# One hand-ordered run of weight units up to the second block, with the later modulation products moved into the feed-forward part

## The chip, the cores and the metric

One core of a Trainium2 chip runs the whole program in one launch. The metric is the device time in microseconds, from the first to the last instruction of an execution, as the median of several executions. Engines: PE is TensorE (matrix products), ACT is ScalarE, DVE is VectorE, POOL is GpSimd, SP issues most transfers. SBUF is the on-chip memory, PSUM the eight banks into which PE writes.

## What is computed

Two model blocks on 256 tokens of width 2048, in float32. The first block is

    a = rms_norm(x); z = a @ w_in                     # 2048 x 4656
    y = concat(rms_norm(rglru(z)), rms_norm(nsa(z)))  # recurrent part and sparse attention
    h = x + rms_norm(y @ w_out)
    f = square(relu(rms_norm(h) @ mlp_w1)) @ mlp_w2   # 2048 x 8192 and back
    h = h + rms_norm(f)
    h = h + sigmoid(h @ ple_gate) * (p @ ple_proj)

and the second has two layers, each on 256 tokens of h and 256 context tokens:

    shift, scale, gate = split(silu(c) @ w_mod[l] + b_mod[l], 3)     # one row for h, one for the context
    z = (rms_norm(x) * (1 + scale) + shift) @ w_in_2[l]              # 2048 x 6656
    y = concat(diff_attention, multiscale_pool, conformer_conv) @ w_out_2[l]
    x = x + gate * y

The modulation vectors depend on `c` and `c_ctx` alone, so their products with `w_mod` (2 x 2048 x 6144) can be made at any time before they are needed.

## The kernel before, in words

**Weight units.** Every large product is cut into chunks of 512 output columns, and each chunk into four units. A unit is a 1 MB piece of weights (512 rows by 512 columns), which SP loads into one of four buffers `raw`. ACT rounds it to `whi` (L1096, L1104, L1352), DVE makes the remainder `wlo = raw - whi` (L1535, L1542, L1900), and PE makes 24 matmuls of 128x128 by 512 from it (4 row tiles, 2 token tiles, and hi*hi, hi*lo, lo*hi; L615 to L617 in `unit`, L656 to L658 in `hand_unit`, L905 to L907 in the feed-forward part). `whi` and `wlo` have two buffers, so ACT may round unit n+1 when PE has used unit n-1. A buffer of `raw` is free when its `wlo` is made (`lo_ready`), and SP then loads the unit four places on.

**Preparation.** `prep` turns normed rows into the stationary operand: PE transposes two column tiles to PSUM (L601), DVE copies them to `tmp` with the column scale (L1527, L1529), ACT rounds that to `hi` (L1089) and POOL subtracts to `lo` (L2141), in 8 groups of 128x512. PE may write the PSUM bank again when DVE has copied it (`t_tmp`).

**Order of the stages.** `HAND` is an order of units written out by hand: 40 units of `in1` with 32 modulation units of layer 0 between them (L742, followed once in five units by a column sum, L732), then 52 units of the context's input product `in2_0c` beside the sparse attention. Modulation units are used by PE straight from `raw`: four fp32 matmuls with 32 columns each, in four column strips of the array. Behind `HAND` the stages follow with a barrier of four engines (`boundary`, L412) between them: `out1` (16 units), the norm and residual `post` (L1139, L1608, L1610) and `prep("mlp")`, the feed-forward part `mlp` (128 units as a loop over four quarters), `post` again, `prep("ple")`, the product with `ple_proj` (L928, fp32), `gate` (16 units), a norm and `prep("m2_00")`, `in2_0` (52 units), and layer 0 of the second block. In `quarter` the rows of the first product are squared by POOL (L2218), transposed by PE (L879) and split by ACT and DVE (L1342, L1873).

**The attention of layer 0** runs 32 batches (L984, L1009, L996 on PE; L1414, L1424 on ACT; L2011, L2024, L2031 on DVE). Between them DVE makes the 31 taps of the convolution (L1991, L1993; one tap a batch in layer 0, two in layer 1), POOL multiplies the gate by its gain once (L2245), and PE makes the remaining 16 groups of modulation products, four units each (`mod_products`, L671), each followed by ACT's copy (L1145), a sum over the strips on PE (`mod_total`, L678), ACT's copy of the row (L1151) and POOL's store to DRAM (L2159). `load_mod` brings the rows of layer 1 back (L2165) to be transposed (L940).

Of the kernel before, what the change touches and what calls it, by code (L numbers as in the profile page):

```python
# [91 lines left out]
def build(nc, I, out):  # L92
    ctx = ExitStack()
    with ctx:
# [27 lines left out]
        vmod = flip[0:64, :]  # L122
        stat = sb("stat", [P, 16])
        epsc = sb("epsc", [P, 1])
# [12 lines left out]
        with region(0) as st:  # L137
# [13 lines left out]
            pT = zst[:, 0, TB].rearrange("p (k t) -> p k t", k=2)  # L151

# [62 lines left out]
        with ExitStack() as st:  # L215
# [12 lines left out]
            modp_b = sb("modp_b", [P, CH], F32, st)  # L228
            modst_b = sb("modst_b", [2, 2, CH], F32, st)
# [31 lines left out]
        class Phase:  # L261
# [10 lines left out]
            Phase("out1", w_out1, 0, 4, 2, "y"),  # L272
            Phase("mlp", None, 0, 8 * FF_Q, 2, "mlp"),
            Phase("pp", None, 0, 4, 2, "pp", split=False),
            Phase("gate", w_gate, 0, 4, 2, "gate"),
            Phase("in2_0", w_in2[0], 0, 13, 2, "z"),
            Phase("mod1", None, 0, len(MODB), 1, "modb", split=False),
# [8 lines left out]
        for ph in PH:  # L286
            ph.r0, ph.s0, ph.c0, ph.z0, ph.p0 = r, s, c, zc, pu
            ph.count = {"s0": s, "c0": c, "z0": zc}
            units = 4 if ph.kind in ("cmp", "pp") else 4 * ph.chunks
            r += units  # L290
            s += units if ph.split else 0
            pu += 0 if ph.split else units
            c += 0 if ph.kind in ("cmp", "mod", "modb", "kept") or ph.name == "in2_0c" else ph.chunks
            zc += ph.chunks if ph.kind == "z" else 0
        BY = {ph.name: ph for ph in PH}

        def after(name, what):
# [9 lines left out]
            dict(name="mix1", src=h, kt=KT, rms=True, mat=eye, xn=xb, hi=ax_hi, lo=ax_lo, off=0, tmp=tmp,  # L307
# [6 lines left out]
                 tmp=G[:, :, :, :].rearrange("p a b c -> p (a b c)")[:, 0:8 * SEQ].rearrange("p (s k t) -> p s k t", k=2, t=SEQ),  # L314
                 scale=lambda k: cols[:, C_GNSA + k:C_GNSA + k + 1], shift=None, units=after("in1g", "s0")),
            dict(name="mlp", src=h, kt=KT, rms=True, mat=eye, xn=xb, hi=ax_hi, lo=ax_lo, off=0, tmp=tmp,
                 scale=lambda k: cols[:, C_MLPPRE + k:C_MLPPRE + k + 1], shift=None, units=after("out1", "s0")),
            dict(name="ple", src=h, kt=KT, rms=False, mat=eye, xn=h, hi=ax_hi, lo=ax_lo, off=0, tmp=tmp,
                 scale=lambda k: ones[:, 0:1], shift=None, units=after("mlp", "s0")),
        ]  # L320
        for l, sm in ((0, 0), (1, 0), (1, 1)):
# [7 lines left out]
        t, nr = 0, 0  # L329
        for pr in PREPS:  # L330
            pr["t0"], pr["r0"] = t, nr
            t += pr["kt"] // 2
            nr += 1 if pr["rms"] else 0
# [10 lines left out]
        class Unit:  # L344

            def __init__(self, ph, i, u, r, s, p):
                self.ph, self.i, self.u, self.r, self.s, self.p = ph, i, u, r, s, p
                self.slot, self.landed = r % UPC, 16 * (r // UPC + 1)

        def laid(order, r, done):  # L350

            out_ = []
            for name in order:
                ph = BY[name]
                k = done.get(name, 0)
                done[name] = k + 1
                out_.append(Unit(ph, k // UPC, k % UPC, r + len(out_), ph.s0 + k if ph.split else None,
                                 None if ph.split else ph.p0 + k))
            return out_

        beside_in1 = []
        for n in range(40):
            beside_in1 += ["in1" if n < 36 else "in1g"] + (["mod0"] if n % 5 < 4 else [])
        beside_nsa = ["in2_0c"] * 4 + ["cmp", "in2_0c"] * 4 + ["in2_0c"] * 44
        done_units = {}
        FIRST = laid(beside_in1, 0, done_units)
        SECOND = laid(beside_nsa, len(FIRST), done_units)
        HAND = FIRST + SECOND
        IN1 = [x for x in FIRST if x.s is not None]
        MOD0 = [x for x in FIRST if x.s is None]  # L370
        CTX0 = [x for x in SECOND if x.s is not None]
        CMP = [x for x in SECOND if x.s is None]
        assert len(HAND) % UPC == 0 and len(HAND) == BY["out1"].r0

        def half(x, b):

            a = (2 * x.i if x.ph.name == "in1" else 18 if x.ph.name == "in1g" else 20 + 2 * x.i) + b
            return a, a % 3
# [108 lines left out]
        for n in ("vec_T", "vec_cols", "cvec_ready", "bias_psum", "bias_row", "bias_out", "lam_dot", "lam_exp",  # L487
                  "lam_ready", "mod_in", "mod_T", "mod_part", "mod_sum", "mod_row", "modp_in", "modc_sum", "modc_set", "x_again", "cvec_zero", "c_T0", "c_copy0",
                  "uc_ready", "pT_psum", "pT_ready", "p_in", "h_in", "lru_w", "bd_zero",
                  "uT_pad", "lru_T", "gT_ready", "xc_ready", "lru_gates", "lru_sig", "lru_ln", "lru_sp", "lru_exp",  # L490
                  "lru_q", "lru_sqrt", "lru_y", "lru_ysq", "lru_ss", "lru_rms", "lru_yn", "lru_hi", "lru_lo",
# [16 lines left out]
        def _(sp):  # L508
# [14 lines left out]
            for n, x in enumerate(HAND):  # L523
# [6 lines left out]
                if x.ph.kind == "cmp":  # L530
                    src = I["cmp_w1_k" if x.u < 2 else "cmp_w1_v"][0].rearrange("(k p) n -> p k n", p=P)
                    sp.dma_start(raw[:, x.slot].rearrange("p a b -> p (a b)").rearrange("p (k n) -> p k n", n=256),
                                 src[:, 8 * (x.u % 2):8 * (x.u % 2) + 8, :]).then_inc(raw_in[x.slot], 16)
                else:
                    sp.dma_start(raw[:, x.slot, :, 0:x.ph.width], x.ph.w[:, UK * x.u:UK * x.u + UK, wcols(x.ph, x.i)])\
                      .then_inc(raw_in[x.slot], 16)
            for ph in PH[PH.index(BY["out1"]):]:
                if ph.kind == "modb":
                    for m_, (l, col) in enumerate(MODB):
                        for u in range(UPC):  # L540
                            free(ph, m_, u)
                            sp.dma_start(raw[:, u], w_mod[l][:, UK * u:UK * u + UK, col * CH:col * CH + CH]).then_inc(raw_in[u], 16)
                elif ph.kind == "pp":
                    for u in range(4):
                        free(ph, 0, u)
                        sp.dma_start(raw[:, u, 0:2, :], I["ple_proj"][0].rearrange("(k p) n -> p k n", p=P)[
                            :, :, u * CH:u * CH + CH]).then_inc(raw_in[u], 16)
                elif ph.kind == "mlp":
                    def quarter(q, first):
                        for j in range(8):  # L550
                            for u in range(UPC):
                                if first and j == 0:
                                    free(ph, 0, u)
                                else:
                                    sp.wait_ge(lo_ready, q * 32 + (ph.s0 + 4 * j - UPC + u + 1))
                                if j < 4:
                                    src = w_up[:, UK * u:UK * u + UK, bass.ds(q * D + j * CH, CH)]
                                else:
                                    src = w_down[:, bass.ds(q * KT + UK * u, UK), (j - 4) * CH:(j - 3) * CH]
                                sp.dma_start(raw[:, u], src).then_inc(raw_in[u], 16)  # L560
                    quarter(0, True)
                    with sp.Fori(1, FF_Q) as q:
                        quarter(q, False)
                else:
# [18 lines left out]
        def _(pe):  # L583
            mm = nc.tensor.matmul

            def prep(name, groups=None):

                if name == "ple":
                    pe.wait_ge(ev("post_done"), 4)
                for g in groups or steps(name):  # L590
# [3 lines left out]
                    if n >= 4:  # L594
                        pe.wait_ge(t_tmp, n - 3)
# [1701 lines left out]
```

## Time and profile before

| what | us |
|---|---|
| median of 3 runs (lowest, highest) | 3214.56 (3213.85, 3218.7) |
| the profiled execution | 3217.97 |
| its span | 3216.3 |
| PE busy | 2849.1 (89%) |
| DVE busy | 1656.3 (51%) |
| ACT busy | 1132.1 (35%) |
| POOL busy | 181.2 (6%) |
| bytes moved, mean rate | 589.21 MB, 183 GB/s |

A busy time is a union over the instructions of an engine, so overlapping matmuls are counted once. The profiled execution took 1.7 us more than its span.

### The profile page before, as it was taken

To read this page: it belongs to the slowest core of one execution; us is meant where nothing else is said; L and a number is where in the kernel's file an instruction comes from. 1 tells how busy PE (TensorE), PEld (TensorE's weight loads), DVE (VectorE), ACT (ScalarE), POOL (GpSimd) and SP (SyncE) were. 2 spreads that over 40 slices of the span, in tenths; PEclk is the share of its full clock that TensorE was granted. 3 is DMA by queue.
4 is the path that set the end of the run, shared out by engine and by line. 5 is a ranking of instruction groups with operands and counts; after the bars stand their busy time and mean duration, and the time that the engine had idled before them with its cause. 6 is when DMAs were issued, how large, how long until landed. Compare 5 with 4: busy or idle time off the path is not lost. (4 is left out here: it accounts for less than half of the span.)

```text
span 3216.3 us, 33116 instructions
## 1 busy us (share of the span) xinstructions
PE 2849.1 (89%) x13308; PEld 2232.7 (69%) x13308; DVE 1656.3 (51%) x1821; ACT 1132.1 (35%) x1321; POOL 181.2 (6%) x176
## 2 busy tenths in 40 slices
PE   4999899998799999999798999787599799996568
PEld 3777788887588888888586887332288678784356
DVE  3644556654554544444544444797533522346954
ACT  3452344433433333333334332343311411232433
POOL 2000100000100000000101000010000200000000
PEclk9999899999899999999899999799799899997789
DMA  6867464464455555555354666799243233464033
GB/s 206 281 236 254 152 232 154 155 223 167 138 187 189 191 187 189 188 187 190 130 190 150 222 221 204 297 339 377 86 149 103 98 128 118 151 221 172 0 135 131
DMA packets 284887, 589.21 MB, mean 183 GB/s; under 512 B 13522, under 2 KB 21562, under 8 KB 282192
## 3 DMA queue, kind: packets, MB, share of 16 engines
q1 hardware_dynamic: 261088, 512.13, 47.1%
q0 software_dynamic: 11552, 48.25, 4.0%
q10 hardware_dynamic: 12112, 26.91, 2.3%
q8 instruction: 100, 1.64, 0.2%
q14 instruction: 35, 0.29, 0.0%
HBM read 560.41 MB, written 26.84 MB: 183 GB/s over the span
## 5 line engine op out<-in xcount | busy, mean ns | idle before, releaser
L1535 DVE TENSOR_TENSOR wlo<-raw,whi 128x2048 fp32r<-128x2048 f32 x170 | 389.0, 2291 | 624.0 <-ACT whi L1096 623.6
L1096 ACT ACTIVATE whi<-raw 128x2048 fp32r<-128x2048 f32 x170 | 325.0, 1915 | 758.1 <-PE ps L617 731.9
L615 PE MATMUL ps<-whi,ax_hi 128*128 128x512 f32 x1344 | 530.4, 395 | 44.8 <-DVE wlo L1535 19.3
L616 PE MATMUL ps<-wlo,ax_hi 128*128 128x512 f32 x1344 | 527.8, 393 | 0.0
L617 PE MATMUL ps<-whi,ax_lo 128*128 128x512 f32 x1344 | 527.5, 392 | 0.0
L1900 DVE TENSOR_TENSOR wlo<-raw,whi 128x2048 fp32r<-128x2048 f32 x126 | 288.8, 2292 | 360.9 <-ACT whi L1352 360.9
L1352 ACT ACTIVATE whi<-raw 128x2048 fp32r<-128x2048 f32 x126 | 241.5, 1917 | 444.9 <-PE ps L907 444.9
L1542 DVE TENSOR_TENSOR wlo<-raw,whi 128x2048 fp32r<-128x2048 f32 (+1 forms) x92 | 203.0, 2207 | 283.5 <-ACT whi L1104 283.2
L615 PEld LDWEIGHTS ps<-whi,ax_hi 128*128 128x128 f32 x1344 | 256.0, 190 | 101.7 <-issue 41.0
L1104 ACT ACTIVATE whi<-raw 128x2048 fp32r<-128x2048 f32 (+1 forms) x92 | 169.8, 1845 | 386.7 <-PE ps L658 229.7
L616 PEld LDWEIGHTS ps<-wlo,ax_hi 128*128 128x128 f32 x1344 | 256.0, 190 | 52.9
L617 PEld LDWEIGHTS ps<-whi,ax_lo 128*128 128x128 f32 x1344 | 255.2, 190 | 53.8
L905 PE MATMUL ps<-whi,ax_hi 128*128 128x512 f32 x512 | 200.7, 392 | 1.9 <-issue 1.9
L905 PE MATMUL ps<-whi,ay_hi 128*128 128x512 f32 x512 | 199.6, 390 | 0.0
L907 PE MATMUL ps<-whi,ax_lo 128*128 128x512 f32 x512 | 199.5, 390 | 0.0
L907 PE MATMUL ps<-whi,ay_lo 128*128 128x512 f32 x512 | 199.3, 389 | 0.0
L906 PE MATMUL ps<-wlo,ax_hi 128*128 128x512 f32 x512 | 199.2, 389 | 0.0
L906 PE MATMUL ps<-wlo,ay_hi 128*128 128x512 f32 x512 | 199.2, 389 | 0.0
L656 PE MATMUL ps<-whi,ay_hi 128*128 128x512 f32 x416 | 167.4, 402 | 6.0 <-DVE wlo L1542 6.0
L658 PE MATMUL ps<-whi,ay_lo 128*128 128x512 f32 x416 | 163.9, 394 | 0.0
L657 PE MATMUL ps<-wlo,ay_hi 128*128 128x512 f32 x416 | 163.5, 393 | 0.0
L1993 DVE SCALAR_TENSOR_TENSOR bv<-uc,cols,bv 128x512 f32<-128x512 f32 (+1 forms) x240 | 140.8, 649 | 0.5
(372 smaller groups left out, 4036.5 us busy)
## 6 DMA issues: line engine op xcount, KB each, us to landing
raw<-in_w_in_dram SPq DMA_DIRECT2D x192, 1024.0 KB, 5.1
raw<-in_mlp_w_dram SPq DMA_DIRECT2D x128, 1024.0 KB, 5.2
raw<-in_w_mod_dram SPq DMA_DIRECT2D x96, 1024.0 KB, 8.5
raw<-in_w_out_dram SPq DMA_DIRECT2D x48, 1024.0 KB, 5.0
raw<-in_ple_gate_dram SPq DMA_DIRECT2D x16, 1024.0 KB, 5.0
z<-zst POOLq DMA_DIRECT2D x22, 512.0 KB, 4.7
z<-zsc POOLq DMA_DIRECT2D x13, 512.0 KB, 3.2
h<-in_x_dram POOLq DMA_DIRECT2D x2, 2048.0 KB, 10.8
```

Of the source, the lines that this page charges most:

```text
L615: mm(dst, hi_[:, kk, tt], whi[:, u % 2, k, 0:width], start=(kk == 0), stop=False)
L616: mm(dst, hi_[:, kk, tt], wlo[:, u % 2, k, 0:width], start=False, stop=False)
L617: ins = mm(dst, lo_[:, kk, tt], whi[:, u % 2, k, 0:width], start=False, stop=(kk == KT - 1))
L905: mm(dst, hi_[:, kk, tt], whi[:, u % 2, k], start=(kk == 0), stop=False)
L906: mm(dst, hi_[:, kk, tt], wlo[:, u % 2, k], start=False, stop=False)
L907: ins = mm(dst, lo_[:, kk, tt], whi[:, u % 2, k], start=False, stop=(kk == KT - 1))
L1096: A(whi[:, u % 2, :, 0:width], raw[:, u, :, 0:width], ACT.Copy).then_inc(hi_ready, 1)
L1104: A(whi[:, x.s % 2, :, 0:w], raw[:, x.slot, :, 0:w], ACT.Copy).then_inc(hi_ready, 1)
L1352: A(whi[:, u % 2], raw[:, u], ACT.Copy).then_inc(hi_ready, 1)
L1535: V.tensor_tensor(wlo[:, u % 2, :, 0:ph.width], raw[:, u, :, 0:ph.width], f32v(whi[:, u % 2, :, 0:ph.width]), ALU.subtract).then_inc(lo_re ...
L1542: V.tensor_tensor(wlo[:, x.s % 2, :, 0:w], raw[:, x.slot, :, 0:w], f32v(whi[:, x.s % 2, :, 0:w]), ALU.subtract).then_inc(lo_ready, 1)
L1900: V.tensor_tensor(wlo[:, u % 2], raw[:, u], f32v(whi[:, u % 2]), ALU.subtract)\
```

## The change

- The hand-written order now runs on to the end of `in2_0`: 48 units of `in2_0c`, the 16 of `out1`, the last 4 of `in2_0c`, the 128 of `mlp` with the 64 modulation units of `mod1` among them (after four of every seven feed-forward units, for 16 x 7 = 112 units), then four times one unit of `ple_proj` and four of `gate`, then the 52 of `in2_0`. The feed-forward loop is written out. The barriers between these stages are gone, and each accumulator of 128x512 is read out by itself, in a ring of three PSUM banks.
- `post` is replaced: ACT squares each chunk as it is read out (`squares`, `down_squares`, `row_squares`), DVE sums and inverts (`rms`), ACT takes the root (`root`), and DVE adds the residual by chunks (`residual`). The norm ahead of `mlp` is applied behind the first product, as the scale `rinv` in its read-out. POOL multiplies the rows of the second norm by their gain. The transposes of `prep("mlp")` stand among the last four units of `in2_0c`.
- `prep` of `mix1`, `nsa`, `mlp` and `ple` has no `tmp`: ACT writes `hi` from PSUM and DVE `lo` from PSUM; POOL has no part. In every `prep`, PE now waits for `a_lo` instead of `t_tmp`.
- The modulation columns of layer 1 are set from PSUM as those of layer 0 are (8 column sums of 4 small matmuls); only the 8 gate rows still go to DRAM. Nothing of `mod1` is left in the attention.

The core of the diff:

```diff
-        beside_nsa = ["in2_0c"] * 4 + ["cmp", "in2_0c"] * 4 + ["in2_0c"] * 44
+        order += ["in2_0c"] * 4 + ["cmp", "in2_0c"] * 4 + ["in2_0c"] * 40
+        order += ["out1"] * 16 + ["in2_0c"] * 4
+        for n in range(128):
+            order += ["mlp"] + (["mod1"] if n < 7 * len(MODB) and n % 7 in (0, 1, 3, 4) else [])
+        order += (["pp"] + ["gate"] * 4) * 4 + ["in2_0"] * 52
...
                     if n >= 4:
-                        pe.wait_ge(t_tmp, n - 3)
+                        pe.wait_ge(a_lo, n - 3)
...
+            for n, x in enumerate(CTX0[48:]):
+                hand_unit(x, AY_)
+                if n in (1, 2):
+                    turned("mlp", 2 * n - 2, 0)
+                    turned("mlp", 2 * n - 1, 0)
...
+                hand_unit(x, AX_ if j < 4 else AY_)
+                m_, at = n // 7, n % 7
+                if m_ < len(MODB) and at in (0, 1, 3, 4):
+                    if at == 0 and m_:
+                        pe.wait_ge(ev("modc_set"), MODSS + before(COLS, m_))
+                        pe.wait_ge(ev("mod_row"), before(ROWS, m_))
+                    mod_products(MOD1[4 * m_ + (0, 1, 0, 2, 3)[at]], 3)
+                elif m_ < len(MODB) and at == 5:
+                    pe.wait_ge(ev("modp_in"), MODSS + m_ + 1)
+                    if m_ in COLS:
+                        mod_columns(modp_b, 3)
+                    else:
+                        mm(ps[0:2, 3, :], sel[:, :], modp_b, start=True, stop=True).then_inc(ev("modc_sum"), 1)
...
+            for i in range(4):
+                turned("ple", i, 4)
+            pe.wait_ge(ev("pT_ready"), 1)
+            for x in GATE:
+                if x.i == 0:
+                    pe.wait_ge(a_lo, PR["ple"]["t0"] + 2 * (x.u + 1))
+                hand_unit(x, AY_)
+                if x.u == 2:
+                    y = PP[x.i]
...
+            pe.wait_ge(gate_mul, 8)
+            for i in range(4):
+                turned("m2_00", i, 8)
+            for x in X0:
+                if x.i == 0:
+                    pe.wait_ge(a_lo, PR["m2_00"]["t0"] + 2 * (x.u + 1))
+                hand_unit(x, AX_)
             boundary(pe, 0)
...
-                    if l == 0 and n and n % 2 == 0 and n <= 2 * len(MODB):
-                        mod_total(n // 2 - 1, modp_b)
...
-                    if l == 0 and n < 2 * len(MODB):
-                        mod_products(n // 2, (0, 1) if n % 2 == 0 else (2, 3))
-                pe.wait_ge(ev("mod_row"), len(MODB))
```

## Rows read from the trace of the kernel before

**Rows 1.** Windows by stage: window, length, PE, PEld, DVE, ACT, POOL, PEclk, DMA, GB/s.
```profile
725.20:735.60 10.40, 1.00 (x6) 0.53 (x4) 3.14 (x3) 3.71 (x2) 0.72 (x1) 0.75 0.13 51
735.60:825.20 89.60, 89.60 (x384) 73.68 (x384) 37.53 (x18) 26.82 (x14) 0.00 (x0) 0.97 0.56 188
825.20:854.40 29.20, 5.60 (x33) 5.57 (x33) 22.27 (x24) 15.30 (x19) 3.31 (x4) 0.59 0.31 108
854.40:1568.20 713.80, 711.88 (x3203) 589.67 (x3201) 345.51 (x180) 258.60 (x146) 37.63 (x22) 1.00 0.56 183
1568.20:1608.60 40.40, 21.45 (x69) 12.91 (x69) 25.48 (x30) 13.35 (x16) 11.19 (x10) 0.78 0.37 129
1698.30:1718.80 20.50, 6.91 (x33) 5.52 (x32) 14.21 (x18) 12.92 (x14) 2.59 (x3) 0.70 0.26 90
2047.40:2241.70 194.30, 156.79 (x961) 57.78 (x961) 165.33 (x327) 86.81 (x262) 18.85 (x20) 0.94 0.98 362
```
**Rows 2.** Timeline of PE in the first stage: start, us, engine, line.
```profile
162.37 1.07 PE L742 MATMUL ps<-raw,cvec 128*32 128x512 f32 x8
163.37 0.50 PE L656 MATMUL ps<-whi,ax_hi 128*128 128x512 f32 x1
...
170.03 0.50 PE L656 MATMUL ps<-whi,ax_hi 128*128 128x512 f32 x1
...
259.77 0.50 PE L656 MATMUL ps<-whi,ax_hi 128*128 128x512 f32 x1
...
266.16 0.48 PE L656 MATMUL ps<-whi,ax_hi 128*128 128x512 f32 x1
```
**Rows 3.** Timeline of DVE in the feed-forward part.
```profile
873.07 2.29 DVE L1900 TENSOR_TENSOR wlo<-raw,whi 128x2048 fp32r<-128x2048 f32 x1 [3.15 <-ACT whi L1352]
878.51 2.29 DVE L1900 TENSOR_TENSOR wlo<-raw,whi 128x2048 fp32r<-128x2048 f32 x1 [3.15 <-ACT whi L1352]
```
**Rows 4.** Groups of instructions: count, busy us, mean ns, idle before and its releaser.
```profile
L678 PE MATMUL ps<-modp_b,sel 128*2 128x512 f32 x32 | 18.0, 647 | 0.7 <-ACT modp_b L1145 0.6
L928 PE MATMUL ps<-raw,zst 128*128 128x512 f32 x32 | 13.9, 592 | 0.0
L671 PE MATMUL ps<-raw,cvec 128*32 128x512 f32 x512 | 68.8, 630 | 21.5 <-DMA raw<-in_w_mod_dram 18.9 <-ACT modst_b L1151 1.8
```
**Rows 5.** Timeline of the attention of layer 0.
```profile
2072.26 0.75 DVE L2024 SCALAR_TENSOR_TENSOR e<-e,st 128x512 f32<-128x512 f32 x1
...
2077.61 0.75 DVE L2024 SCALAR_TENSOR_TENSOR e<-e,st 128x512 f32<-128x512 f32 x1
...
2140.98 11.60 DVE L1993 SCALAR_TENSOR_TENSOR bv<-uc,cols,bv 128x512 f32<-128x512 f32 x4
2141.15 8.88 POOL L2245 TENSOR_TENSOR k<-k,subg 128x4096 f32<-128x4096 f32 x1
...
2153.73 0.48 DVE L2024 SCALAR_TENSOR_TENSOR e<-e,st 128x256 f32<-128x256 f32 x1
...
2158.28 0.48 DVE L2024 SCALAR_TENSOR_TENSOR e<-e,st 128x256 f32<-128x256 f32 x1
...
2226.55 0.69 DVE L2011 TENSOR_REDUCE st<-ps 128x2 f32<-128x512 f32 x1 [0.94 <-PE ps L984]
...
2236.24 0.35 DVE L2031 TENSOR_SCALAR q<-ps,st 128x128 f32<-128x128 f32 x1 [1.10 <-PE ps L996]
```
**Rows 6.** A window of layer 1's attention, which has no modulation products.
```profile
2980.00:3000.00 20.00, 13.16 (x57) 8.20 (x55) 19.55 (x47) 6.67 (x21) 0.00 (x0) 0.66 0.00 0
```
**Rows 7.** Timeline of a preparation with POOL.
```profile
336.25 10.01 POOL L2141 TENSOR_TENSOR ay_lo<-zsc,ay_hi 128x512 fp32r<-128x512 f32 x8 [0.64 <-ACT ay_hi L1089]
```
**Rows 8.** SP's issues behind the product of 162.37, and the rounding they allow.
```profile
163.91 0.51 SPq L535 DMA_DIRECT2D raw<-in_w_in_dram  x1
...
172.52 1.92 ACT L1104 ACTIVATE whi<-raw 128x2048 fp32r<-128x2048 f32 x1 [8.07 <-DMA raw<-in_w_in_dram]
```
**Rows 9.** DMA issues by tensor: count, KB each, median us to landing.
```profile
raw<-in_mlp_w_dram SPq DMA_DIRECT2D x128, 1024.0 KB, 5.2
```

More of the change, by code:

```diff
@@ new lines, in build, with of @@
+        HAND = laid(order)
+        SPLIT = [x for x in HAND if x.s is not None]
+        def of(name):
+            return [x for x in HAND if x.ph.name == name]
+        IN1, MOD0, CTX0, CMP, PP = of("in1") + of("in1g"), of("mod0"), of("in2_0c"), of("cmp"), of("pp")
+        MOD1 = of("mod1")
+        OUT1, MLP, GATE, X0 = of("out1"), of("mlp"), of("gate"), of("in2_0")
+        assert len(HAND) % UPC == 0 and len(HAND) == BY["out2_0"].r0
+        ROWS = [m_ for m_, (l, col) in enumerate(MODB) if col >= MODSS]
@@ L536, in _ @@
                       .then_inc(raw_in[x.slot], 16)
[L537 to L564, printed above, removed]
+            for ph in PH[PH.index(BY["out2_0"]):]:
+                if ph.chunks:
                     def body(i, odd, ph=ph):
@@ L1324, in _ @@
             beside = Beside(nsa())
[L1325 removed]
+            for n, x in enumerate((CTX0[0:48] + OUT1[0:2])[2:]):
                 hand_split(x)
                 beside(n)
[L1328 to L1338 removed]
@@ L1355, in _, with squares @@
-            quarter(0, True)
-            with act.Fori(1, FF_Q) as q:
-                quarter(q, False)
-            boundary(act, 1)
-            post(1, yb, after("mlp", "c0"))
-            prep("ple")
-            gemm("gate", gate=True)
+            def squares(xs, i, n):
+                for b in range(TB):
+                    a, bank = half(chunk(xs, i)[0], b)
+                    act.wait_ge(unit_used, chunk(xs, i)[3].s + 1) if b else act.wait_ge(half_done, a // 2 + 1)
+                    A(yb[:, b, i * CH:i * CH + CH], ps[:, bank, :], ACT.Square, accum_out=ssq[:, n, b, i:i + 1])\
+                        .then_inc(ev("post_sq"), 1)
@@ new lines, in _, with sigmoids @@
+            hand_split(GATE[0])
+            down_squares(3)
+            root(2)
+            hand_split(GATE[1])
+            prep("ple")
+            def sigmoids(i):
+                for b in range(TB):
+                    a, bank = half(chunk(GATE, i)[0], b)
+                    act.wait_ge(unit_used, chunk(GATE, i)[3].s + 1) if b else act.wait_ge(half_done, a // 2 + 1)
+                    if i >= 2:
+                        act.wait_ge(gate_mul, 2 * (i - 2) + b + 1)
+                    A(zst[:, i % 2, b], ps[:, bank, :], ACT.Sigmoid).then_inc(half_out, 1)
@@ new lines, in _ @@
+            for n, x in enumerate((OUT1 + CTX0[48:] + MLP[0:2])[2:]):
+                if n < 16 and n % 4 == 3:
+                    gained(n // 4)
+                if n == 19:
+                    to_memory(CTX0, 12)
+                hand_low(x)
+                if n == 15:
+                    rms(0, 0, 8)
+                    dve.wait_ge(ev("x_again"), 16)
+                    residual(0, 0)
+                    residual(0, 1)
+                if n == 16:
+                    residual(0, 2)
+                    residual(0, 3)
+                if n in (17, 18):
+                    prep("mlp", range(4 * n - 68, 4 * n - 64))
```

708 lines of the change are left out of this document (371 added, 337 removed).

## The prediction

> **What bounds the kernel now.** Read the windows by stage first [rows 1]. In the feed-forward part (854.4 to 1568.2) PE is busy 711.9 of 713.8 us at the full clock of 2.4 GHz (PEclk 1.00): whatever is added to PE's stream there lengthens the run by its whole price. Between the stages lie holes in which PE does little: 10.4 us ahead of `out1`, 29.2 ahead of `mlp`, 40.4 ahead of `gate`, 20.5 ahead of `in2_0`. Layer 0's attention (194.3 us) is another kind of stage: PE 156.8 us, DVE 165.3 us. Its timeline [rows 5] decides which of the two sets the pace. Where nothing is late, DVE's step at L2024 recurs every 5.35 us (2072.26 to 2077.61) for the batches of 512 keys and every 4.55 us (2153.73 to 2158.28) for those of 256, and DVE has no idle time ahead of these rows. So over long stretches the modulation products run beside DVE's work for nothing. The change fills the holes, which is a gain, and takes 64 products from a stage in which most of them are free to one in which none is.
>
> **The cost of the products on PE.** The first stage already mixes weight units and products in this manner. From 163.37 to 170.03 there is one unit and one product, 6.66 us [rows 2]; a unit alone has a pitch of 5.44 us, 873.07 to 878.51 [rows 3]. One product costs 1.22 us: 64 x 1.22 = 78.1 us. A unit with a column sum takes 266.16 - 259.77 = 6.39 us [rows 2], so a sum costs 0.95 us: 8 x 0.95 = 7.6. The 8 row sums are two records of L678 each, 18.0 us for 16 of them [rows 4], 1.1 us, and I add 0.2 us for entering and leaving as the product shows (1.22 against 68.8 / 64 = 1.08 busy [rows 4]): 8 x 1.3 = 10.4. The four transposes of `p`, until now in a hole, go in too: about 1.1. Together 97.2 us. Bounds: 90 (row sums at 1.0, nothing for entering) and 106 (next paragraph).
>
> **The weights' arrival.** The products hold buffers of `raw` until PE has used them. The tight case of the first stage is in [rows 2, 8]: the product of 162.37 frees a buffer, SP issues two transfers, the second at 163.91, and ACT can round that unit at 172.52, 10.15 us after the product began. Another 4.3 us of ACT and DVE (L1104, 1.92 there, and 2.29 [rows 3]) make 14.5 us, against the 14.5 that PE needs for product, unit, product, unit and product; PE hardly waits. In the new order the fourth and the fifth unit of each seven come first behind such a release, without a second megabyte ahead, and land in about 5.2 us [rows 9]: 1.1 + 5.2 + 4.3 = 10.6 us, against two products and two units, 13.3 us, that PE has to do before each. I take 1 us of waiting over the stage; the bound above is 0.5 us at one place of each of 16 groups. ACT's copy, DVE's column settings (0.15 to 0.2 us each) and POOL's stores lie inside a unit's 5.44 us; if that cover fails, PE waits at `modc_set` or `mod_row`, once a group.
>
> **What the holes give back.** *Ahead of `out1`*: 725.2 to 825.2 holds 16 units, 100.0 us against 87.0 at the pitch of 5.44; this counts 2.5 us of low clock in the first units (PEclk 0.97). Gain 12.8 (the last matmul ends at about 725.4). *Ahead of `mlp`*: 29.2 us, of which 5.6 are the transposes, which stay. The four held-back units cover the norm: after the last unit of `out1`, DVE has a weight's remainder, sum and inverse, two residual chunks (1.4 us each), and the next remainder, which comes about 1.5 us too late. Gain 21.9; bounds 17 and 24. *Ahead of `gate`*: counted from the end of the last feed-forward unit, DVE adds the last half (0.7), ACT squares it (0.8), sum, root and inverse take 1.0, then DVE in one row makes four residuals (5.6), six of the eight parts of `lo` (0.7 each) and one remainder (2.3); the last transposes end at about 15 us. The products with `ple_proj` (13.9 us [rows 4]), until now inside the hole, come between the units of `gate`, at the same price. 40.4 - 15 - 13.9 = 11.5 gained; bounds 4 and 16. *Ahead of `in2_0`*: the squares of the last chunks, a root with its table, four scalings, and then POOL's parts of 1.25 us (10.01 / 8 [rows 7]) with PE waiting for each: about 18.9 us in place of 20.5. Gain 1.6, bounds -3 and 5.
>
> **What else costs.** The wait for `a_lo` ties PE to POOL's pace in the preparations that keep `tmp`: in [rows 7] the fifth to eighth group would be transposed only after POOL's first to fourth, the last some 5 us behind POOL's start and so about 2.9 us later than now. I take 2.9 us there, 2 in layer 1, and 0.8 for `mix1`, where DVE's 0.95 us a group replaces POOL's 1.25 us. Together 5.7, bounds 0 and 9. What goes in layer 1 with `load_mod` is a transpose beside ACT's squares: 0.5 gained.
>
> **The attention.** Without products, count on DVE: from 2072.26 (batch 4) twelve steps of 5.35 lead to batch 16 (0.5 less for its shorter maximum), then fifteen of 4.55 [rows 5]. To that comes one stall. At 2140.98 four taps take 11.60 us in place of 2.73, while POOL's gain product (L2245) runs for 8.88: 8.9 us, and the change leaves that product in. The last maximum then starts at 2072.3 + 63.7 + 68.3 + 8.9 - 1.3 = 2211.9, against 2226.55, 14.6 earlier. Behind it the last results come 9.7 us later now, 2 to 3 of them for products and waits on them, so some 17 us in all. Bounds: 12 and 26. Layer 1 shows this limit at work [rows 6]: without products DVE is busy 19.55 of 20 us.
>
> The stall bears out a rule of the Trainium skill ("SBUF — State Buffer", Terms and "SBUF: two separate sides"): one port pair serves DVE and GpSimd, held for a whole instruction, the loser blocked. It speaks against part of the change, since POOL now multiplies yb by the gain beside DVE's residuals: at some 1 us for the last two it would make the hole ahead of `gate` up to 2 us longer.
>
> The clock falls in this stage: 0.94 now, and 0.66 in the layer without products [rows 1, 6], a mixture of 2.4 and 1.2 GHz. DVE stays the bound there in spite of it; I count up to 1 us of it, in the tail. The Trainium skill ("TensorE: Matmul & The Clock Gate", Part 1) says the same of an engine that is little used; by its two speeds the matmuls would take twice as long, which would eat the gain only if they led.
>
> **The sum.** Gains 12.8 + 21.9 + 11.5 + 1.6 + 0.5 + 17 = 65.3. Costs 97.2 + 1 + 5.7 = 103.9. The changed kernel is 38.6 us slower: 3256.6 against the profiled 3217.97. That execution is 3.4 us above the median of 3214.56, so I forecast **3253 us**. All gains at their best and costs at their least (88 against 90) give no change; the other way (46 against 115) gives 69 more. They won't all fall together.
>
> **Rivals.**
> 1. *The attention gives back all of PE's time.* If PE led there, it would shorten by 68.8 + 18.0 = 86.8 us [rows 4] in place of 17, and the kernel would come to 3253 - 70 = 3183, faster. PE's 81% and 21.5 us of waiting for weights speak for it, the even steps of 5.35 and 4.55 us against it. It decides the sign from 56 us on. Chance 0.06.
> 2. *Weights come late in the feed-forward part.* If the fourth and fifth unit of each seven waited behind another megabyte, as the 10.15 us of the first stage show, they would be ready 14.5 us behind the release instead of 10.6, 1.2 us too late each, 2.4 a group: 16 x 2.4 = 38, so 3291. Half of it, 3272, if only one of the two does. For it: the transfers share one queue. Against: these two are first in it. Chance 0.12.
> 3. *The holes don't close as worked out*, since the chain from the last read-out over ACT, DVE and PE has hand-overs that I count at nothing: half of the 33 us ahead of `mlp` and `gate` is lost, 3270. Chance 0.12.
> 4. *The change keeps less than it says*: the products are in the new place but hide in gaps of PE's pitch (0.23 us a matmul against 0.21 of 512 columns at 2.4 GHz). The first stage shows 1.22 us for each, so no. With half of the 97 us hidden the kernel would be faster, 3205. Chance 0.03.
>
> **How the numbers follow.** The forecast has 0.67. The range takes its own spread of 15 us to either side, rival 3 and the milder form of rival 2: 3232 to 3284. A measurement of this kernel can tell about 0.2%, 6.4 us, from no change. Faster: rivals 1 and 4, and little of the forecast's lower tail, 0.09. Within 0.2% (up to 3221): only that tail, 0.04. Slower: 0.87.
>
> **What would show it.** Right: PE busy nearly throughout the feed-forward part, that part about 97 us longer; windows of about 15 us ahead of `gate` and 19 ahead of `in2_0`; no hole ahead of `out1`; an attention of some 177 us with DVE over 90% busy and a PE clock near 0.7. Wrong: PE waits on `wlo` or on DMA twice in seven units (rival 2); an attention under 140 us (rival 1); waits on L1089 or on residuals ahead of the transposes that sum to over 20 us (rival 3).

## The result, and the profile after

The changed kernel takes 3289.43 us (median of 4 runs, 3287.78 to 3295.1) against 3216.27 (3213.85 to 3218.7) for the kernel before on the same chip: a ratio of 1.0234, 95% interval 1.0221 to 1.0247. It is 73 us slower, where 39 were forecast. The direction was right, and the time lies 5 us above the range.

The windows by stage of the changed kernel, in order: `out1`; the four held-back units with the transposes ahead of `mlp`; `mlp`; the hole ahead of `gate`; `gate` with the products of `ple_proj`; the hole ahead of `in2_0`; layer 0's attention up to DVE's last result. They answer to [rows 1], whose `out1` and `mlp` holes were 10.4 and 29.2 us.

```profile
703.40:790.40 87.00, 87.00 (x385) 72.06 (x384) 41.81 (x24) 35.15 (x31) 0.72 (x1) 1.00 0.59 199
790.40:815.70 25.30, 25.30 (x129) 21.29 (x128) 20.68 (x29) 19.07 (x39) 0.00 (x0) 1.00 0.60 179
815.70:1621.90 806.20, 806.16 (x3797) 602.23 (x3795) 359.47 (x240) 276.47 (x183) 51.39 (x49) 1.00 0.74 252
1621.90:1636.60 14.70, 6.96 (x33) 5.93 (x34) 12.82 (x19) 7.10 (x13) 2.50 (x2) 0.67 0.00 0
1636.60:1786.70 150.10, 112.27 (x417) 84.99 (x415) 44.75 (x31) 36.87 (x32) 0.00 (x0) 0.86 0.38 136
1786.70:1806.50 19.80, 6.46 (x33) 5.84 (x33) 16.68 (x25) 9.57 (x17) 5.41 (x5) 0.69 0.18 58
2132.60:2302.90 170.30, 103.69 (x416) 65.97 (x416) 160.42 (x316) 67.65 (x226) 10.12 (x2) 0.65 0.04 13
```

Read the lengths against those of before. The span grew by 71.9 us (3216.3 to 3288.2); the changes are taken before rounding:

| stretch | before | after | change | forecast |
|---|---|---|---|---|
| up to the first unit of `out1`, 52 and 48 units of `in2_0c` | 725.4 | 703.4 + 21.8 | -0.2 | +3.7 |
| hole ahead of `out1`, and `out1` | 99.8 | 87.0 | -12.8 | -12.8 |
| ahead of `mlp`, without the four units | 29.2 | 25.3 - 21.8 = 3.5 | -25.7 | -21.9 |
| `mlp` | 713.8 | 806.2 | +92.4 | +98.2 |
| hole ahead of `gate` and, before, `ple_proj` | 40.4 | 14.7 | -25.7 | -25.4 |
| `gate` (after: with `ple_proj`) | 89.7 | 150.1 | **+60.4** | **+13.9** |
| hole ahead of `in2_0` | 20.5 | 19.8 | -0.7 | -1.6 |
| `in2_0` and the loads | 328.6 | 326.1 | -2.5 | 0 |
| attention, up to the start of DVE's last result | 188.8 | 170.3 | -18.6 | -17 |
| the rest | 980.1 | 985.3 | +5.3 | +1.5 |

The forecast column is the prediction's sum of +38.6 laid out by these stretches (the wait for `a_lo` is 0.8 and 2.9 in the first, 2 in the last; the 13.9 of `ple_proj` move from the hole to `gate`). One line carries the miss: `gate` took 46.5 us more than worked out, and the sum of all others came out 13 us better.

PE's waits in that stretch are a single row:

```profile
PE ps L662 <- DVE wlo L1607: 37.8, 4, 9.5
```

Four waits of about 9.5 us, one for each chunk. The timelines of PE, SP, ACT and DVE around the first of them show how it comes about:

```profile
1653.14 3.59 PE L935 MATMUL ps<-raw,zst 128*128 128x512 f32 x8
1666.25 0.76 PE L662 MATMUL ps<-whi,ay_hi 128*128 128x512 f32 x1 [9.51 <-DVE wlo L1607]
1666.81 0.63 PE L663 MATMUL ps<-wlo,ay_hi 128*128 128x512 f32 x1
...
1671.08 0.50 PE L664 MATMUL ps<-whi,ay_lo 128*128 128x512 f32 x1
1671.42 0.39 PE L662 MATMUL ps<-whi,ay_hi 128*128 128x512 f32 x1
```
```profile
1656.77 0.37 SPq L569 DMA_DIRECT2D raw<-in_ple_gate_dram  x1
```
```profile
1661.87 1.91 ACT L1115 ACTIVATE whi<-raw 128x2048 fp32r<-128x2048 f32 x1 [17.43 <-DMA raw<-in_ple_gate_dram]
```
```profile
1663.81 2.29 DVE L1607 TENSOR_TENSOR wlo<-raw,whi 128x2048 fp32r<-128x2048 f32 x1 [17.05 <-ACT whi L1115]
```

The order of units is one `ple_proj`, then four of `gate`. The `ple_proj` unit lies in a buffer `raw` until PE has used it, and PE uses it behind the third unit of `gate`. The unit four places on, which needs this buffer, is the fourth of `gate`: PE's very next work. SP issues its load at 1656.77, when the product ends; it lands 5.1 us later (ACT starts at 1661.87), ACT and DVE take their 1.9 and 2.3, and PE starts at 1666.25. The 12 matmuls behind the wait then come at a pitch of 0.43 us instead of 0.23, half the clock of 2.4 GHz: 5.17 us (1666.25 to 1671.42) for what takes 2.72 at the full rate, so 2.5 us more; behind the other three waits it is 5.29 us, 2.6 more. These stretches are part of why PEclk is 0.86 in that window.

In the attention DVE's steps at L2128 are those of [rows 5], 5.35 us from the third step on and 4.55 us in the batches of 256 keys, with shorter ones of 4.82 where the two kinds meet, and with one long one, beside POOL's gain product:

```profile
2182.07 0.75 DVE L2128 SCALAR_TENSOR_TENSOR e<-e,st 128x512 f32<-128x512 f32 x1
2183.00 11.31 DVE L2097 SCALAR_TENSOR_TENSOR bv<-uc,cols,bv 128x512 f32<-128x512 f32 x4
...
2196.00 0.75 DVE L2128 SCALAR_TENSOR_TENSOR e<-e,st 128x512 f32<-128x512 f32 x1
```
```profile
2183.74 9.35 POOL L2347 TENSOR_TENSOR k<-k,subg 128x4096 f32<-128x4096 f32 x1 [49.83 <-ACT k L1487]
```

### The profile page after: what moved, and what is told of

Read it like the earlier page. It is cut to its first block and busy times, and to the rows that moved or that the text cites. A ratio compares the mean times of both kernels' runs of the same rounds, so it can differ in the third digit from the quotient of the medians.

```text
span 3288.2 us, 32257 instructions
## 1 busy us (share of the span) xinstructions
PE 2897.6 (88%) x13355; PEld 2257.9 (69%) x13355; DVE 1653.4 (50%) x1895; ACT 1132.8 (34%) x1381; POOL 159.2 (5%) x162
## 5 line engine op out<-in xcount | busy, mean ns | idle before, releaser
L1607 DVE TENSOR_TENSOR wlo<-raw,whi 128x2048 fp32r<-128x2048 f32 x304 | 688.9, 2267 | 970.4 <-ACT whi L1115 970.1
L662 PE MATMUL ps<-whi,ax_hi 128*128 128x512 f32 (+1 forms) x1376 | 543.9, 395 | 0.2 <-DVE wlo L1607 0.2
L664 PE MATMUL ps<-whi,ax_lo 128*128 128x512 f32 (+1 forms) x1376 | 534.1, 388 | 0.0
L663 PE MATMUL ps<-wlo,ax_hi 128*128 128x512 f32 (+1 forms) x1376 | 533.7, 388 | 0.0
L1600 DVE TENSOR_TENSOR wlo<-raw,whi 128x2048 fp32r<-128x2048 f32 x84 | 192.3, 2292 | 385.8 <-ACT whi L1107 385.4
L621 PE MATMUL ps<-whi,ax_hi 128*128 128x512 f32 x672 | 265.7, 395 | 32.1 <-DVE ay_lo L2207 13.5
L662 PEld LDWEIGHTS ps<-whi,ay_hi 128*128 128x128 f32 x1056 | 202.6, 192 | 110.0 <-DVE wlo L1607 37.5
L622 PE MATMUL ps<-wlo,ax_hi 128*128 128x512 f32 x672 | 263.8, 393 | 0.0
L623 PE MATMUL ps<-whi,ax_lo 128*128 128x512 f32 x672 | 263.6, 392 | 0.0
L664 PEld LDWEIGHTS ps<-whi,ay_lo 128*128 128x128 f32 x1056 | 201.9, 191 | 44.0
L663 PEld LDWEIGHTS ps<-wlo,ay_hi 128*128 128x128 f32 x1056 | 202.7, 192 | 40.4
```

The costliest lines, as they stand in the source:

```text
L621: mm(dst, hi_[:, kk, tt], whi[:, u % 2, k, 0:width], start=(kk == 0), stop=False)
L622: mm(dst, hi_[:, kk, tt], wlo[:, u % 2, k, 0:width], start=False, stop=False)
L623: ins = mm(dst, lo_[:, kk, tt], whi[:, u % 2, k, 0:width], start=False, stop=(kk == KT - 1))
L662: mm(dst, hi_[:, kk, tt], whi[:, x.s % 2, k, 0:w], start=(kk == 0), stop=False)
L663: mm(dst, hi_[:, kk, tt], wlo[:, x.s % 2, k, 0:w], start=False, stop=False)
L664: ins = mm(dst, lo_[:, kk, tt], whi[:, x.s % 2, k, 0:w], start=False, stop=(kk == KT - 1))
```

## The experiments

Times are medians, ratios those to the kernel before on the same chip with 95% intervals. "e1", "e3" and so on are the labels of the runs.

**e1_order and e2_use_first: is it the buffer, and its release?**

```diff
-        order += (["pp"] + ["gate"] * 4) * 4 + ["in2_0"] * 52
+        order += (["gate"] * 3 + ["pp", "gate"]) * 4 + ["in2_0"] * 52
```
```diff
-                if x.u == 2:
+                if x.u == 0:
                     y = PP[x.i]
```

> The changed kernel with one line other: the order of the gate part is three units of gate, the ple_proj unit, the fourth unit of gate, instead of the ple_proj unit first. All arithmetic and all of PE's order stay. Theory A (the ple_proj unit holds its raw buffer until PE has used it behind the third gate unit, so the load of the fourth gate unit is issued only then, PE waits 9.3 to 9.5 us for wlo four times and restarts at half clock): four waits of about 9.5 us go, and with each some 3 us of matmuls at 1.2 GHz; 3289 - 38 - 11 = about 3241 us, gate stage about 102 us instead of 150.1. Rival B (the fp32 products between gate units, or DVE's extra work, slow the stage whatever the loads do): within 10 us of 3289.

> The changed kernel with the order of the loads as it is, but PE uses the ple_proj buffer behind the first of the four gate units instead of the third. Theory A: the buffer is freed two units (10.9 us) earlier; from the release the fourth gate unit needs about 0.4 us (issue) + 5.6 (landing) + 1.9 + 2.3 (ACT, DVE) + hand-overs, some 13 us as 1653.1 to 1666.3 of the changed kernel's trace shows from the product's start, of which 3.6 are the product: 9.5 us behind it, against the 10.9 us of two units. So nearly all of the waits goes here too: 3243 us, between 3238 and 3255. Rival B: no change, 3289. If only the place of the unit in the load order mattered and not the time of its release, e1 would gain and this would not.

e1: 3242.74 us, 1.0079 (1.0063 to 1.0094). e2: 3240.19 us, 1.0075 (1.0060 to 1.0091). Either edit takes back 47 to 49 us, all that the forecast missed and some more. The windows of e1 for `gate` and the hole behind it:

```profile
1636.10:1737.60 101.50, 101.49 (x418) 78.37 (x416) 44.89 (x31) 37.04 (x33) 0.00 (x0) 1.00 0.49 165
1737.60:1757.40 19.80, 6.38 (x33) 5.77 (x33) 16.65 (x25) 9.57 (x17) 5.38 (x5) 0.72 0.40 137
```

101.5 us in place of 150.1, PE busy throughout, at full clock. Of the 48.6 us, 37.8 are the waits; of the other 10.8 some 10 are the restarts at half clock (2.5 once and 2.6 three times). PE's instructions and their order are the same in e1 as in the changed kernel, so rival B (the fp32 products themselves slow the stage) is out. In e2 the order of the loads is that of the changed kernel, and only the release comes earlier; it gains as much, and PE waits for no `wlo` in that stage. So it is the time of the release, not the place in the queue.

What one product of `ple_proj` costs is seen from its start to the unit behind it, here in e1:

```profile
1652.92 3.59 PE L935 MATMUL ps<-raw,zst 128*128 128x512 f32 x8
1655.95 0.79 PE L662 MATMUL ps<-whi,ay_hi 128*128 128x512 f32 x1
1656.59 0.40 PE L663 MATMUL ps<-wlo,ay_hi 128*128 128x512 f32 x1
```

The second matmul of the unit stands 3.67 us behind the product's start, where 0.23 would be the pitch without it: 3.4 us for each, 13.8 for the four. The stage is only 101.5 - 89.7 = 11.8 us longer than before, since its first units ran at half clock then (PEclk 0.97, 89.7 us for the 87.0 of 16 units) and hardly do now.

**e3_back: the products back in the attention, the run without barriers kept**

```diff
-            order += ["mlp"] + (["mod1"] if n < 7 * len(MODB) and n % 7 in (0, 1, 3, 4) else [])
+            order += ["mlp"]
...
+                    if l == 0 and n < 2 * len(MODB):
+                        late_products(n // 2, (0, 1) if n % 2 == 0 else (2, 3))
```

(With them went back `mod_total`, the copies, the stores and `load_mod` of the kernel before; the order of e1 was kept.)

> e1 with the 64 modulation products of mod1 and their sums back in the attention of layer 0, as in the kernel before (rows to DRAM and back); the run without barriers stays. Theory: the feed-forward part loses the 92.4 us that it grew by (806.2 to 713.8, or some 3 less), the attention gets back the 18.6 us that it lost: 3241 - 92 + 19 = about 3168 us, 1.5% faster than the kernel before (range 3160 to 3178). Rival (part of the holes was only closed because the products held PE busy while ACT and DVE caught up, or the weights come late without them): 3180 to 3200. Rival (the products in the attention cost more next to the barrier-free run, whose tail in DRAM traffic reaches into it): up to 3180.

3165.34 us, 0.9844 (0.9830 to 0.9857): 1.6% faster than the kernel before. Windows of `mlp` and of the attention:

```profile
810.00:1523.80 713.80, 713.80 (x3217) 592.39 (x3216) 359.45 (x221) 267.49 (x168) 47.36 (x41) 1.00 0.60 191
...
1989.80:2178.60 188.80, 155.40 (x960) 57.32 (x960) 162.11 (x316) 84.80 (x258) 17.76 (x18) 0.95 0.99 362
```

Both are back at their lengths of before, 713.8 us and 188.8 (counted to the end of DVE's last result; 188.4 to its start), and every hole stays as small as it was with the products, so that gain doesn't hang on them. Moving the products costs 92.4 - 18.6 = 74 us by the windows and 77 by e1 against e3; the run without barriers, with `ple_proj` in the right place, gains 50.

**e4_half_loads: what do the products cost in the attention?**

```diff
-                            sp.dma_start(raw[:, u], w_mod[l][:, UK * u:UK * u + UK, col * CH:col * CH + CH]).then_inc(raw_in[u], 16)
+                            sp.dma_start(raw[:, u, 0:2], w_mod[l][:, UK * u:UK * u + 2, col * CH:col * CH + CH]).then_inc(raw_in[u], 16)
```

> e3 with only half of each 1 MB piece of w_mod loaded in the attention (32 MB in place of 64 MB); all instructions on all engines stay, the products read what was left in the other half of the buffer, so their values are left out of the computation. e3's attention, from the first score matmul to the last L2154, takes 1989.8 to 2178.55 = 188.8 us; the kernel without products there takes 170.25. Theory (what the products cost there is the transfer: DVE's steps of 5.42 us in the batches of 256 keys are 2 MB at 387 GB/s, against DVE's own 4.55): the steps go back to 4.55 and the attention to 171 to 175 us; the kernel to about 3150. Rival (PE's own time with its hand-overs to ACT's copies sets the 5.42): the attention stays within 3 us of 188.8.

3153.35 us, 0.9808 (0.9780 to 0.9837). The products read what the other half of the buffer held before, so this kernel leaves out half of the sums of these products; the instructions are those of e3. A window of 60 us in the batches of 256 keys, first of e4, then of e3:

```profile
2100.00:2160.00 60.00, 53.52 (x370) 19.81 (x362) 57.85 (x132) 29.22 (x110) 3.52 (x7) 1.00 0.73 242
```
```profile
2100.00:2160.00 60.00, 47.95 (x308) 15.73 (x306) 51.07 (x116) 24.49 (x94) 3.05 (x6) 0.98 0.97 354
```

With half the bytes PE does more in the same time (370 matmuls against 308), and DVE is busy 57.9 of 60 us again. The attention takes 174.9 us in place of 188.8: 14 of the 18 us that the products cost there go with the bytes. DVE's step, again first in e4, then in e3:

```profile
2121.77 0.49 DVE L2147 SCALAR_TENSOR_TENSOR e<-e,st 128x256 f32<-128x256 f32 x1
2126.32 0.48 DVE L2147 SCALAR_TENSOR_TENSOR e<-e,st 128x256 f32<-128x256 f32 x1
```
```profile
2121.07 0.48 DVE L2147 SCALAR_TENSOR_TENSOR e<-e,st 128x256 f32<-128x256 f32 x1
2126.49 0.49 DVE L2147 SCALAR_TENSOR_TENSOR e<-e,st 128x256 f32<-128x256 f32 x1
```

The 5.42 us of e3 are two pieces of 1.05 MB at 387 GB/s; in e4 the step is 4.55 again. PE's waits for `w_mod`, 19.7 us in e3's attention and 18.9 in the kernel before, are gone in e4. Of the other 4 us, 3.2 lie in one step of 8.51 us in place of 5.35 that e4 keeps (it ends at 2053.60; DVE waits 2.47 us in it for PE's scores); what in the products causes it was not taken apart.

**e5_pieces: is DVE held by POOL's instruction, or by POOL's work?** The gate product in 32 instructions of 128 columns, on e1, where DVE alone sets the pace.

```diff
-                    nc.gpsimd.tensor_tensor(g3, g3, subg[:, :].unsqueeze(1).broadcast_to([P, nq * H2, P]), ALU.mult)
+                    for c_ in range(nq * H2):
+                        ins = nc.gpsimd.tensor_tensor(g3[:, c_], g3[:, c_], subg[:, :], ALU.mult)
```

> e1 with POOL's product of the gate with its gain (one instruction over 4096 columns, 8.88 us, during which DVE's taps stand still) cut into 32 instructions of 128 columns. Theory (DVE's operations that read SBUF alone wait for POOL's instruction to end, and DVE sets the pace there): DVE is held only piece by piece, in all by about POOL's time or more, since each piece has its own fixed cost: the one step of 13.9 us is spread over several, the attention stays at 170 us +-3. Rival (between the pieces DVE gets its turn while it reads PSUM or is at its small operations, so that POOL's work hides): the steps stay at 5.35 and the attention takes 162 to 165 us.

3234.93 us, 1.0057 (1.0034 to 1.0079). The attention takes 165.4 us against 170.1 in e1 (to the start of DVE's last result): that is between the theory (at least 167) and the rival (at most 165), and all but at the rival. POOL and DVE in e5:

```profile
2134.44 21.18 POOL L2348 TENSOR_TENSOR k<-k,subg 128x128 f32<-128x128 f32 x32 [49.84 <-ACT k L1487]
```
```profile
2133.70 3.13 DVE L2097 SCALAR_TENSOR_TENSOR bv<-uc,cols,bv 128x512 f32<-128x512 f32 x4
2136.75 1.21 DVE L2115 TENSOR_REDUCE st<-ps 128x2 f32<-128x1024 f32 x1
```

POOL is busy without a gap and DVE goes on beside it, so they take turns: POOL needs 21.2 us for what it does in 9.35 in one instruction, and DVE's four taps 3.13 and 3.33 us in place of 2.73. The four longer steps (6.06, 6.49, 6.43, 6.11) add up to 3.7 us more than 5.35 each, where the single instruction cost 8.6.

**e6_tmp_wait and e7_scale_first: two small holes**, both on e3.

```diff
+                    if pr["tmp"] is not None and g >= 4:
+                        pe.wait_ge(t_tmp, pr["n0"] + g - 3)
```
```diff
                 ins.then_inc(ev("post_done"), 1)
-                if i:
-                    prep("m2_00", range(2 * i - 2, 2 * i))
-            prep("m2_00", range(6, 8))
+            prep("m2_00")
```

> e3 with PE in the preparations that keep tmp waiting again for DVE's copy of the group four back (t_tmp) instead of POOL's remainder (a_lo). Theory: the 7.4 us in one wait of L607 on POOL ax_lo in layer 1's preparation, and some of m2_00's and m2_01's, go; the ends of these preparations come 3 us earlier in layer 1 and up to 3 in m2_01, kernel 3 to 5 us faster than e3, some 3161. Rival (DVE waits for a_lo itself before it writes tmp again, so only the place of the wait changes): within 1 us of e3 in each of the three preparations.

> e3 with DVE's eight scalings ahead of in2_0 (L2030, SBUF to SBUF) done before the first copy of the preparation, instead of two ahead of each pair of groups. In the changed kernel the second and third pair of them take 2.87 and 2.86 us beside POOL's remainders, the first two pairs 1.67 together. Theory (they stand still while POOL works, DVE's copies from PSUM do not): the eight take 3.3 us in one row, and the hole ahead of in2_0 shrinks from 19.8 to about 17 us. Rival (POOL then starts later by what the scalings take, and PE waits for its remainders instead): the hole stays within 1 us of 19.8.

e6: 3160.46 us, 0.9831 (0.9802 to 0.9859). e7: 3160.83 us, 0.9832 (0.9803 to 0.9860). The two runs each are too few to tell 5 us by time alone; the traces show the places. In e6 the transposes of layer 1 go from 2456.3 to 2500.4, in e3 from 2460.5 to 2507.9: 3.3 us less. Their waits, e3 first:

```profile
  POOL ax_lo L2264: 7.4, 1
```
```profile
  DVE tmp L1608: 5.3, 1
```

Those of m2_01 take 6.05 us in one row against 8.7, which is 2.7 less. So the wait for `a_lo` cost 2.7 us there and 3.3 in layer 1, where 2.9 and 2 were forecast.

In e7 the hole is 17.4 us (1642.4 to 1659.8) in place of 19.8. DVE in the changed kernel, then DVE and POOL in e7:

```profile
1793.38 1.67 DVE L2030 TENSOR_SCALAR yb<-h,rinv 128x512 f32<-128x512 f32 x4
1795.49 1.90 DVE L1594 TENSOR_SCALAR tmp<-ps,modc 128x256 f32<-128x256 f32 x4 [0.44 <-PE ps L607]
1797.31 2.87 DVE L2030 TENSOR_SCALAR yb<-h,rinv 128x512 f32<-128x512 f32 x2
1800.11 1.89 DVE L1594 TENSOR_SCALAR tmp<-ps,modc 128x256 f32<-128x256 f32 x4
```
```profile
1649.11 3.26 DVE L2040 TENSOR_SCALAR yb<-h,rinv 128x512 f32<-128x512 f32 x8
...
1656.56 0.99 DVE L1606 TENSOR_SCALAR tmp<-ps,modc 128x256 f32<-128x256 f32 x2 [0.57 <-PE ps L608]
```
```profile
1654.01 9.92 POOL L2262 TENSOR_TENSOR ax_lo<-tmp,ax_hi 128x512 fp32r<-128x512 f32 x8 [126.24 <-ACT ax_hi L1113]
```

In the changed kernel POOL makes two remainders from 1797.23 to 1799.90, and the two scalings from SBUF to SBUF that fall there take 2.87 us instead of 0.83. In e7 POOL is busy without a gap from 1654.01, and DVE's copies out of PSUM go on beside it at 0.5 us each. The Trainium skill ("SBUF — State Buffer", "SBUF: two separate sides") says that the pair of ports shared with GpSimd is taken by DVE operations with two SBUF inputs or in a two-port mode, and by no others. The trace agrees if the scalings, which have one tensor input, run in such a mode: they slowed from 0.83 to 2.87 us for two, and the copies out of PSUM did not.

**e9_no_cover: what are the four held-back units worth?** The 52 units of `in2_0c` ahead of `out1` again, on e3.

```diff
-        order += ["in2_0c"] * 4 + ["cmp", "in2_0c"] * 4 + ["in2_0c"] * 40
-        order += ["out1"] * 16 + ["in2_0c"] * 4
+        order += ["in2_0c"] * 4 + ["cmp", "in2_0c"] * 4 + ["in2_0c"] * 44
+        order += ["out1"] * 16
```

> e3 with the four units of in2_0c that were held back moved ahead of out1 again: no work of PE stands between the last unit of out1 and the transposes of the preparation ahead of the feed-forward part; no barrier comes back. Theory (the four units cover the norm's chain, and are all that makes this hole vanish where the one ahead of gate keeps 14.7 us): PE is idle but for the transposes for about 14 to 15 us there instead of 3.5, and restarts at half clock for about 2 us; 3165 + 12 = 3177 us. Rival (taking the barrier away and reading out by halves closes most of the hole, the units little): under 5 us more than e3.

3182.38 us, 0.9889 (0.9871 to 0.9908). PE behind `out1`:

```profile
823.26 3.68 PE L608 MATMUL ps<-eye,h 128*128 128x128 f32 x16 [6.95 <-DVE h L1946]
828.39 1.97 PE L608 MATMUL ps<-eye,h 128*128 128x128 f32 x8 [1.46 <-DVE h L1946]
831.28 1.97 PE L608 MATMUL ps<-eye,h 128*128 128x128 f32 x8 [0.92 <-DVE h L1946]
```

PE's last unit ends at 816.3 and the next begins at 832.9: a hole of 16.6 us in place of 3.5, and behind it six matmuls at half clock. The cover is worth 14 to 17 us (by the ratios and by the medians); without barriers but without cover the hole is near the 14.7 us of the one ahead of `gate`. So of the 25.7 us that this hole gave back, 29.2 - 16.6 = 12.6 come from the missing barriers and the new `post` (no run parts these two), the other 13.1 from the four units.

**e8_all, e10_spread, e11_two: the gains together**

> e3 with three things together that gained alone: POOL's gate product in 32 pieces (e5, 4.7 us of the attention), the wait of the preparations on DVE's copy instead of POOL's remainder (e6, 2.9 us in m2_01 and 3.3 in layer 1), the scalings ahead of in2_0 in one row (e7, 2.4 us). If they add up: 3165 - 13 = 3152 us. The pieces may bring less here than in e1, since transfers set part of the attention's pace (e4): then 3154 to 3157. With t_tmp PE no longer waits for POOL ahead of in2_0 either, so that hole may go under the 17.7 us of e7.

> e8 with the 32 pieces of POOL's gate product spread over the attention: four behind each of POOL's stores of a modulation row from the eighth to the fifteenth. In the profiled run of e8 the 32 pieces ran back to back in 13.24 us and one tap of DVE stood still for 13 us, in e5 they took 21.18 us and DVE lost 3.7 us in all; e8's five times fall in two groups (3144 to 3146, 3158 to 3161) about that far apart. Theory (whichever of the two engines holds the port may keep it over a row of short instructions; four in a row are at most 1.7 us): one group of times, no step of DVE longer by more than 2 us, and since the batches of 256 keys have some 0.9 us of slack each behind the transfers, most of it hidden: 3146 to 3151 us. Rival (the cost follows POOL's whole time, wherever it runs): 3157 us as e11.

> e3 with the wait on DVE's copy (e6) and the scalings in one row (e7), the gate product left as one instruction. The two are local and in different places: 3165 - 6.2 - 2.4 = 3157 us, between 3154 and 3159, in one group of times; the hole ahead of in2_0 at most 17.7 us.

| run | median | lowest, highest | ratio |
|---|---|---|---|
| e8: e6 + e7 + the 32 pieces | 3146.39 | 3144.38, 3161.24 | 0.9786 (0.9764 to 0.9808) |
| e11: e6 + e7 | 3155.40 | 3149.55, 3158.87 | 0.9817 (0.9801 to 0.9834) |
| e10: e8 with four pieces behind each of eight stores | 3147.05 | 3144.07, 3149.79 | 0.9796 (0.9782 to 0.9809) |

e8 was faster than expected by its median, but two of its five times (3157.96, 3161.24) are 12 to 17 us above the others, and its profiled execution is one of them. POOL and DVE there:

```profile
2077.07 13.24 POOL L2359 TENSOR_TENSOR k<-k,subg 128x128 f32<-128x128 f32 x32
```
```profile
2077.24 15.61 DVE L2116 SCALAR_TENSOR_TENSOR bv<-uc,cols,bv 128x512 f32<-128x512 f32 x4
```

The same 32 instructions that took turns with DVE in e5 ran back to back here, 13.24 / 32 = 0.41 us each, and DVE's four taps took 15.6 us. In e10 no step of DVE is more than 2 us above its usual one where a piece runs, the attention takes 181.6 us against 189.1 in e11, and its five times lie within 5.7 us. e11's spread of 9.3 us speaks against a reading of e8's two groups by POOL alone; that is left open. e10 is 2.0% faster than the kernel before and 4.3% faster than the changed one (0.9796 / 1.0234).

## Why the prediction was wrong, and where it was right

- **The step that failed**: "The products with `ple_proj` (13.9 us [rows 4]), until now inside the hole, come between the units of `gate`, at the same price." Their price on PE was right (13.8 us by the rows of e1). What was left out is the buffer: a unit used in another place than its place in the order of loads holds its slot meanwhile. The prediction worked out just this for the modulation products ("hold buffers of `raw` until PE has used them"), found it harmless there, and did not ask it of the other plain units, one stage on. Measured: 48.6 us go with e1, four waits of 9.3 to 9.5 us for `wlo` and the half clock behind them; the stage grew by 60.4 us, 46.5 more than the step's own 13.9 (the last 2.1 are the better start of the stage).
- **Rival 2** had the mechanism and the wrong place. In `mlp` PE waits for nothing at all (806.16 of 806.2 us busy); the 1 us taken for it was too much, though the median landing of an `mlp` weight went from 5.2 [rows 9] to 6.5 us. In `gate` it cost 12 us at each of four places, where the rival had 1.2 at each of 32. That its 3291 us lies 2 us from the measured time is chance.
- **The products' cost**: 92.4 us for 97.2 + 1. The row sums take 0.95 us like the column sums, not 1.3 (16 records of L910, 8.2 us busy), which is 2.8; the rest of the difference, about 2 us beside the 1 of waiting, was not traced. e3 shows the same total by taking them out (806.2 to 713.8).
- **The holes**: ahead of `out1` 12.8 as worked out; ahead of `mlp` 25.7 instead of 21.9, above the bound of 24, since no part of the norm's chain comes late behind four units (PE busy 25.30 of 25.30 us) and the transposes run at full clock; ahead of `gate` 14.7 us for 15; ahead of `in2_0` 19.8 for 18.9. Rival 3 is out: it had some 17 us lost ahead of `mlp` and `gate`, and these two came out 4 us better. What the prediction feared from the shared port ahead of `gate`, up to 2 us, is 0.3: POOL's last gain products run from 1622.19 to 1624.69, DVE's four residuals begin at 1624.10 and take 3.12 us, where later pairs take 1.41.
- **The attention**: 18.6 us for 17, DVE busy 160.4 of 170.3 us, PEclk 0.65, one stall of 8.6 us: the count of DVE's steps held, and with it the answer to rival 1 (PE's time is not what is given back). What it did not see is why the products cost anything there: it weighed PE against DVE, and the third candidate, the transfers, stood in its own [rows 1] with a DMA share of 0.98 and 362 GB/s. e4 shows them to be 14 of the 18 us. That the products "run beside DVE's work for nothing" held for most batches of 512 keys; of the 15 steps of 256 keys in the kernel before, six in a row took 5.41 to 5.45 us:

```profile
2184.12 0.48 DVE L2024 SCALAR_TENSOR_TENSOR e<-e,st 128x256 f32<-128x256 f32 x1
2189.55 0.48 DVE L2024 SCALAR_TENSOR_TENSOR e<-e,st 128x256 f32<-128x256 f32 x1
```

- **The preparations**: `a_lo` cost 2.7 and 3.3 us for 2.9 and 2 (e6). `mix1` did not cost its 0.8: a wait of PE of 4.1 us for `wlo` behind that preparation, in the kernel before, is gone (why was not traced). Some 3 us of that gain were lost again ahead of `out1`, beyond `a_lo`'s 2.7, also by a cause not traced.
- **Smaller sums**: in `in2_0` 2.5 us went that were not forecast, and the stages behind the attention took 5.3 us more for 1.5; 1.3 of that difference is layer 1's `a_lo`, the rest was not traced. The bounds that the prediction states for its gains add up to 84 and 43 us, not to its 88 and 46; the forecast doesn't rest on them.

The terms apart from `gate` came out 13 us better than the sum and `gate` 46.5 us worse, of which 33 remain. Without the waits in `gate` (e1) the time is 3243 us, inside the range and 10 us under the forecast.

## What to carry to other kernels

When a buffer ring is filled in one order and used in another, write down for each slot which load waits for its release and how long before its use that load is issued; the unit's place in the list and PE's place of use must be moved together (here one line, 48 us). Before work is moved off a stage, ask what that stage is bound by, and count the transfers among the candidates: 64 products cost 18.6 us, most of it as transfers, beside a DVE-bound attention and 92.4 us in a PE-bound stage, so the half of a change that closes holes can be worth 50 us (67 with two small repairs and the spread pieces) while the half that moves work hides it. Taking a barrier away and reading out by chunks closed about half of the hole ahead of `mlp` (12.6 of 25.7 us); the rest took independent units held back for it.

## What the hardware did that was not expected

- **Who keeps the shared port is not settled by the length of the instructions.** The 32 short POOL instructions alternated with DVE's taps in e5 (21.18 us, DVE loses 3.7) and shut them out in e8 (13.24 us, DVE loses 13). The Trainium skill ("SBUF — State Buffer", "SBUF: two separate sides") says that whichever starts first has the pair for its whole instruction. For rows of short instructions these two runs show both outcomes; what decides between them was not found. Groups of four bound the loss (e10, under 2 us a step).
- **A wait costs PE more than its length.** Behind each wait of 9.5 us, 12 matmuls ran at half clock, 2.5 to 2.6 us more for each wait, about a quarter on top; the hole of e9 restarts at half clock too, for six matmuls.
- **One core drew 387 GB/s** over 50 us of e3's attention, while the mean of the whole program is 186, so a stage can be bound by transfers where the mean gives no hint of it. The row of GB/s by slices, on the page of the kernel before, shows it with 339 and 377. The window of e3:

```profile
2000.00:2050.00 50.00, 43.29 (x264) 16.83 (x264) 46.25 (x89) 27.86 (x63) 2.06 (x4) 0.95 1.05 387
```
